# LayerNorm 1 to the first gather in token halves, with the routing ranked by comparison

## The reference

```python
mod = cond @ w_ada[l] + b_ada[l]              # sh1, sc1, gt1, sh2, sc2, gt2
...                                           # mixer: mLSTM heads and a short convolution
x = layer_norm(ALPHA * x + (1 + gt1) * mix, ln1_g[l], ln1_b[l])
u = x * (1 + sc2) + sh2
grp_logits = u @ w_grp + b_grp                # 4 groups
grp_idx = argmax(grp_logits)
exp_logits = u @ w_router + b_router          # 4 experts in each group
top_vals, top_idx = top_k(exp_logits[grp_idx], 2)
top_w = softmax(top_vals) * softmax(grp_logits)[grp_idx]
y = sum over the 2 experts of top_w * (silu(u @ w_gate) * (u @ w_up)) @ w_down
x = layer_norm(ALPHA * x + (1 + gt2) * y, ln2_g[l], ln2_b[l])
```

## Time and profile before

| | us |
|---|---|
| three runs | 889.2, 884.86, 888.09; median 888.09 |
| profiled execution | 891.73 |
| its span | 889.9 |
| PE busy | 825.8 (93%) |
| DVE busy | 338.7 (38%) |
| ACT busy | 100.2 (11%) |
| DMA moved | 299.29 MB, 336 GB/s over the span |
| mean granted TensorE clock | 0.958 |

### The profile page before, as it was taken

How to read it: one execution, slowest core, us unless ns; L and a number is a source line. 1 busy time by engine, 2 the same in 40 slices (tenths; PEclk the granted TensorE clock), 3 DMA queues, 4 the chain that set the end, 5 groups by cost and what they waited for, 6 DMA issues and landing times.

```text
span 889.9 us, 9042 instructions
## 1 busy us (share of the span) xinstructions
PE 825.8 (93%) x3753; PEld 439.6 (49%) x3753; DVE 338.7 (38%) x807; ACT 100.2 (11%) x222; POOL 28.4 (3%) x69
## 2 busy tenths in 40 slices
PE   5899999969999999999979999998799999999991
PEld 2585686445344443443347658745444443444330
DVE  0169848653121012110253985676521112101106
ACT  2111000012011110110111100001111101111010
POOL 2060000000000000000000000000000000000000
PEclk9999999969999999999969999997899999999996
DMA  8999994284999999999999699336399999999961
GB/s 301 390 343 387 387 332 178 94 355 158 389 411 414 414 414 410 415 414 412 394 387 395 244 385 376 115 148 244 149 387 413 414 414 409 415 414 414 410 259 49
DMA packets 90653, 299.29 MB, mean 336 GB/s; under 512 B 4152, under 2 KB 4440, under 8 KB 82416
## 3 DMA queue, kind: packets, MB, share of 16 engines
q1 hardware_dynamic: 86960, 291.60, 84.2%
q0 software_dynamic: 2592, 7.04, 2.1%
q10 hardware_dynamic: 1056, 0.03, 0.1%
HBM read 297.60 MB, written 1.05 MB: 336 GB/s over the span
## 4 chain that ended last, share of the span: by engine, by line
PE 84%; DVE 4%; DMA 4%; SPq 4%; issue 2%; ACT 1%; ACTq 0%; DVEq 0%
PE bank L548 23%; PE bank L506 16%; PE bank L572 12%; PE bank L535 7%; PE bank L713 6%; PE bank L523 6%; PE bank L592 6%; SPq L335 3%; DMA ring<-in_w_ada_dram 2%; DMA ring<-in_w_in_dram 2%; PE bank L455 1%; PE bank L479 1%; PE bank L556 1%; SPq L331 1%; ACT uT L795 1%
## 5 line engine op out<-in xcount | busy, mean ns | idle before, releaser
L506 PE MATMUL bank<-uT,ring 128*128 128x256 f32 x640 | 142.6, 384 | 0.5 <-DMA ring<-in_w_in_dram 0.5
L506 PEld LDWEIGHTS bank<-uT,ring 128*128 128x128 f32 x640 | 122.6, 193 | 21.2 <-issue 3.5
L548 PE MATMUL bank<-ring,qT 128*64 128x512 f32 x512 | 113.1, 594 | 2.8 <-issue 2.8
L572 PE MATMUL bank<-ring,hb 128*64 128x512 f32 x512 | 113.4, 595 | 1.4 <-ACT hb L821 1.4
L548 PE MATMUL bank<-ring,uT 128*64 128x512 f32 x512 | 112.7, 594 | 0.0
L572 PEld LDWEIGHTS bank<-ring,hb 128*64 128x64 f32 x512 | 35.3, 137 | 76.4 <-issue 74.6
L548 PEld LDWEIGHTS bank<-ring,qT 128*64 128x64 f32 x512 | 36.8, 137 | 70.9 <-issue 69.9
L548 PEld LDWEIGHTS bank<-ring,uT 128*64 128x64 f32 x512 | 36.0, 137 | 70.8 <-issue 68.5
L535 PEld LDWEIGHTS bank<-ccT,X 128*128 128x128 f32 x512 | 62.5, 198 | 13.4 <-issue 13.4
L535 PE MATMUL bank<-ccT,X 128*128 128x128 f32 x512 | 64.9, 286 | 0.0
L935 DVE SCALAR_TENSOR_TENSOR acc<-ring,cond,acc 128x512 f32<-128x512 f32 x84 | 63.1, 752 | 3.0
(11 more groups left out here) (227 smaller groups left out, 564.3 us busy)
## 6 DMA issues: line engine op xcount, KB each, us to landing
ring<-in_w_gate_dram SPq DMA_DIRECT2D x32, 2048.0 KB, 17.0
ring<-in_w_up_dram SPq DMA_DIRECT2D x32, 2048.0 KB, 16.3
ring<-in_w_down_dram SPq DMA_DIRECT2D x32, 2048.0 KB, 15.6
ring<-in_w_ada_dram SPq DMA_DIRECT2D x24, 2048.0 KB, 19.8
ring<-in_w_in_dram SPq DMA_DIRECT2D x14, 2048.0 KB, 18.9
ring<-in_w_out_dram SPq DMA_DIRECT2D x4, 2048.0 KB, 14.2
gate_row<-in_b_ada_dram POOLq DMA_DIRECT2D x4, 512.0 KB, 7.7
ln_g<-in_ln_g_dram POOLq DMA_DIRECT2D x4, 512.0 KB, 10.5
```

What stands on the lines that cost most here:

```text
L506: last = pe.matmul(bank[4 + (b0 + q) % 4][:, 0:SEQ], w[:, kc, q * P:(q + 1) * P], uT[:, kc, :], start=(kc == 0), stop=(kc == KC - 1))
L548: last = pe.matmul(bank[bk][CAP * j:CAP * (j + 1), :], xg[b][:, 4 * h + k, CAP * j:CAP * (j + 1)], ring[s[h]][:, 4 * j + k, :], start=(h = ...
L572: last = pe.matmul(bank[6 + half][CAP * j:CAP * (j + 1), :], hhT[:, f, CAP * j:CAP * (j + 1)], ring[s[h]][:, 4 * j + 2 * i + half, :], sta ...
```

## The change

- Extractions 4 and 5 go ahead of the head transposes, 8 and 9 between these and the output projection; `shift_scale` goes ahead of `residual_norm`.
- The last block of the output projection (tile 1, half 1) is made in two blocks of 256 columns, in banks 3 and 7; LayerNorm's `add` follows it in two rounds.
- Transposes, modulation, route matmuls and fold are done for tokens 0 to 127 and then for 128 to 255, the first half's in parts on ScalarE alone.
- The routing compares every logit with each of its row of four, ranks them by the counts, and makes the mask (bf16) from the ranks. What only the weights need (`dif`, scores, `best`) comes behind the dispatch matrix.
- Clearing of banks 0 to 3 and the extractions of gate 2 stand ahead of the wait for the mask; two position matmuls in bf16 replace three in float32.
- `disp` and `dispw` are one instruction each of 256 columns; `dispw` is `disp` times the weight. Positions count from 1, so one subtraction is gone.

```diff
@@ -694,6 +713,8 @@
                 pe.wait_ge(proj_dve, 8 * l + 8)
                 ada_extract(l, GATE1)
                 ada_extract(l, GATE1 + 1)
+                ada_extract(l, 4)
+                ada_extract(l, 5)
 
                 pe.wait_ge(h_ready, l + 1)
                 pe.wait_ge(gate_row_ready, 4 * l + 2)
...
@@ -704,41 +725,46 @@
                     if h % 2:
                         last.then_inc(hT_done, 1)
+                ada_extract(l, 8)
+                ada_extract(l, 9)
                 pe.wait_ge(hT_copied, 2 * (l + 1))
                 for half in range(2):
                     arrived(pe, l, WOUT_UNIT[half])
                     w = ring[slot(l, WOUT_UNIT[half])]
                     for t in range(T):
-                        for kc in range(KC):
-                            last = pe.matmul(bank[2 * t + half][:, :], mixT[:, kc, t * P:(t + 1) * P], w[:, kc, :],
-                                             start=(kc == 0), stop=(kc == KC - 1))
-                        last.then_inc(mix_done, 1)
-                for i in (4, 5, 8, 9):
-                    ada_extract(l, i)
-                pe.wait_ge(x_ready, 2 * T * l + T)
-                transpose_x(x_ready, 2 * T * l + 1, 1, rows_of)
-                pe.wait_ge(uT_act, 8 * l + 8)
+                        for to, cols in blocks_of(t, half):
+                            for kc in range(KC):
+                                last = pe.matmul(to, mixT[:, kc, t * P:(t + 1) * P], w[:, kc, cols],
+                                                 start=(kc == 0), stop=(kc == KC - 1))
+                            last.then_inc(mix_done, 1)
+                transpose_half(l, 0)
+                pe.wait_ge(mod_ready, 2 * l + 2)
+                clear_quarters(6)
+                pe.wait_ge(uT_act, 16 * l + 12)
+                pe.wait_ge(route_landed, 16 * 10 * DEPTH)
+                in_quarters(6, w_route_sb[:, l, :, :], logT_done, slice(0, P))
+                transpose_half(l, 1)
+                pe.wait_ge(logT_act, l + 1)
+                pe.matmul(bank[6][:, SEQ:SEQ + G + EXPERTS], quarters[:, 0:P], fold[:, :], start=True, stop=True)
+                pe.wait_ge(uT_act, 16 * l + 16)
                 pe.wait_ge(uT_dve, 8 * l + 8)
-                pe.wait_ge(route_landed, 16 * 10 * DEPTH)
-                in_quarters(6, w_route_sb[:, l, :, :], logT_done)
+                in_quarters(6, w_route_sb[:, l, :, :], logT_done, slice(P, SEQ))
+                pe.wait_ge(logT_dve, l + 1)
+                pe.matmul(bank[6][:, SEQ + 32:SEQ + 32 + G + EXPERTS], quarters[:, P:SEQ],
+                          fold[:, :], start=True, stop=True).then_inc(logit_done, 1)
                 for b in range(4):
                     pe.matmul(bank[b][:, :], zeros[:, 0:P], zeros[:, :], start=True, stop=False, skip_group_check=True)
-                pe.wait_ge(logT_copied, l + 1)
-                for t in range(T):
-                    last = pe.matmul(bank[6][:, SEQ + 32 * t:SEQ + 32 * t + G + EXPERTS], quarters[:, t * P:(t + 1) * P],
-                                     fold[:, :], start=True, stop=True)
-                last.then_inc(logit_done, 1)
-                pe.wait_ge(mask_ready, l + 1)
-                pe.matmul(bank[6][:, 0:EXPERTS], before[:, :], mask[:, 0, :], start=True, stop=True)
-                pe.matmul(bank[6][:, EXPERTS:2 * EXPERTS], ones[:, :], mask[:, 0, :], start=True, stop=False)
-                pe.matmul(bank[6][:, EXPERTS:2 * EXPERTS], before[:, :], mask[:, 1, :],
-                          start=False, stop=True).then_inc(pos_done, 1)
                 ada_extract(l, GATE2)
                 ada_extract(l, GATE2 + 1)
+                pe.wait_ge(mask_ready, l + 1)
+                pe.matmul(bank[6][:, 0:2 * EXPERTS], before[:, :], mask[:, :, :].rearrange("p t e -> p (t e)"),
+                          start=True, stop=False, skip_group_check=True)
+                pe.matmul(bank[6][:, EXPERTS:2 * EXPERTS], all_ones[:, :], mask[:, 0, :],
+                          start=False, stop=True, skip_group_check=True).then_inc(pos_done, 1)
                 gather(main, PAIRS * l, 0)
...
@@ -962,22 +1005,33 @@
+            def residual_norm(l, which):
+                    blocks = [(bank[2 * t + half][:, :], slice(0, COLS))]
+                        blocks = blocks_of(t, half)
+                    for i, (src, cols) in enumerate(blocks):
+                        if which == 0:
+                            dve.wait_ge(mix_done, 5 * l + 2 * half + t + i + 1)
+                        to = slice(half * COLS + cols.start, half * COLS + cols.stop)
+                        n = cols.stop - cols.start
+                        link(dve.tensor_tensor(tmp[:, 0:n], src, gate_row[:, to], ALU.mult))
+                        link(dve.scalar_tensor_tensor(out=X[:, t, to], in0=X[:, t, to], scalar=ALPHA,
+                                                      in1=tmp[:, 0:n], op0=ALU.mult, op1=ALU.add))
+                        if which == 0 and t == T - 1:
+                            for q in range(to.start // SEQ, to.stop // SEQ):
+                                last = dve.bn_stats(stats[:, t, q, :], X[:, t, q * SEQ:(q + 1) * SEQ])
+                        else:
+                            last = dve.bn_stats(stats[:, t, half, :], X[:, t, to])
+                        link(last)
+                    n = 4 if which == 0 and t == T - 1 else 2
+                    link(dve.bn_aggr(mv[:, t, :], stats[:, t, 0:n, :].rearrange("p a b -> p (a b)")))
...
@@ -1006,41 +1060,25 @@
+                two_of = slice(e0, e0 + 2) if isinstance(e0, int) else bass.ds(e0, 2)
+                dve.tensor_tensor(disp[b][:, :, :].rearrange("p t (e s) -> p t e s", e=2),
+                                  slots[:, :].unsqueeze(1).unsqueeze(1).to_broadcast([P, T, 2, CAP]),
+                                  pos[:, :, two_of].unsqueeze(3).to_broadcast([P, T, 2, CAP]), ALU.is_equal).then_inc(S.disp, 1)
+            def build_dispw(S, n, e0, b):
+                two_of = slice(e0, e0 + 2) if isinstance(e0, int) else bass.ds(e0, 2)
+                dve.wait_ge(S.disp, n + 1)
+                dve.tensor_tensor(dispw[b][:, :, :].rearrange("p t (e s) -> p t e s", e=2),
+                                  disp[b][:, :, :].rearrange("p t (e s) -> p t e s", e=2),
+                                  comb[:, :, two_of].unsqueeze(3).to_broadcast([P, T, 2, CAP]), ALU.mult).then_inc(S.dispw, 1)
+            def build(S, n, e0, b):
+                build_dispw(S, n, e0, b)
...
@@ -1201,63 +1239,73 @@
+                shift_scale(l)
+                residual_norm(l, 0)
+                modulate_half(l, 1, range(4, KC))
+                dve.wait_ge(logT_done, 2 * l + 2)
+                dve.tensor_copy(quarters[:, P:SEQ], bank[6][:, P:SEQ]).then_inc(logT_dve, 1)
+                el = logit[:, :, G:G + EXPERTS]
+                rows = logit[:, :, :].rearrange("p t (n e) -> p (t n) e", e=E)
+                N = T * (1 + G)
+                link(dve.tensor_tensor(ahead[:, :, :, :], rows.unsqueeze(2).to_broadcast([P, N, E, E]),
+                                       rows.unsqueeze(3).to_broadcast([P, N, E, E]), ALU.is_ge))
+                link(dve.tensor_tensor(ahead[:, :, :, :], ahead[:, :, :, :],
+                                       lower[:, :, :].unsqueeze(1).to_broadcast([P, N, E, E]), ALU.mult))
+                dve.tensor_reduce(rank[:, :, :], ahead[:, :, :, :], AX.X, ALU.add)
+                link(dve.tensor_reduce(behind[:, :, :], ahead[:, :, :, :].rearrange("p n i j -> p n j i"), AX.X, ALU.add))
+                link(dve.tensor_tensor(rank[:, :, :], rank[:, :, :], behind[:, :, :], ALU.subtract))
+                want = last_rank[:, :].unsqueeze(1).to_broadcast([P, N, E])
+                dve.scalar_tensor_tensor(out=two[:, :, :, :].rearrange("p t n e -> p (t n) e"), in0=rank[:, :, :], scalar=-1.0,
+                                         in1=want, op0=ALU.add, op1=ALU.is_le)
+                link(dve.tensor_tensor(first[:, :, :, :].rearrange("p t n e -> p (t n) e"), rank[:, :, :], want, ALU.is_equal))
+                group = first[:, :, 0, :].unsqueeze(3).to_broadcast([P, T, G, E])
+                dve.tensor_tensor(mask[:, :, :].rearrange("p t (g e) -> p t g e", g=G), two[:, :, 1:1 + G, :], group,
+                                  ALU.mult).then_inc(mask_ready, 1)
+                dve.wait_ge(mask_ready, l + 1)
+                dve.tensor_tensor(chosen1[:, :, :, :], first[:, :, 1:1 + G, :], group, ALU.mult)
+                link(dve.tensor_reduce(best[:, :, 0:1], gl, AX.X, ALU.max))
+                dve.tensor_tensor(dif[:, :, 0:G], gl, best[:, :, 0:1].to_broadcast([P, T, G]), ALU.subtract)
+                link(dve.tensor_tensor(chosen2[:, :, :, :], mask[:, :, :].rearrange("p t (g e) -> p t g e", g=G),
+                                       chosen1[:, :, :, :], ALU.subtract))
+                build_disp(main, 0, 0)
```

(61 more changed lines are left out.)

123 lines of the change are left out of this document (36 added, 87 removed).

## The result

The changed kernel takes 879.78 us (median of 20 runs, 875.79 to 889.67) against 883.62 us for the kernel before (20 runs). The ratio is 0.994, interval 0.9918 to 0.9962: 5.3 us faster (3.4 to 7.2). It leaves out two slow runs of the changed kernel and so is further from 1 than the ratio of the medians as they stand, which differ by 3.8 us. A second set gives 0.9935 (0.9906 to 0.9963), 5.8 us. The forecast was 10.5 us. The direction was right, but the gain is half of the forecast. That the time of 879.78 us lies even in the likeliest case's 874 to 880 is luck: the forecast started from the median of three runs, 888.09, and over 20 runs the kernel before has 883.62.

What follows compares the result with a forecast made beforehand. TensorE (busy 93%) was taken as the bound, except some 25 us per layer between output projection and gather. Gains of 7.75 and 7.4, less 2 x 2.25 and 0.1, gave 10.5 us: 877.6 from 888.09, range 873 to 884.

Steps and rivals of the forecast that it cites:

- the likeliest case: The whole kernel, no rival coming true: 877.6 us, own range 874 to 880, chance 0.64.
- Time saved here reaches the end: Between output projection and gather: a microsecond saved in either layer counts as one of the span.
- The extractions, +2.25 per layer: Extractions 4, 5, 8 and 9, moved ahead of the output projection, lengthen the path by 2.25 us per layer.
- The split: Last output projection block as 16 matmuls of 256 columns for 8 of 512: costs nothing, at most 0.1 us.
- the low clock at the projection: Rival: the clock falls near 150 and the projection's start runs at half; 3.4 us lost per layer, 884.4 us; chance 0.08.
- LayerNorm, logits, routing: M + 5.25, 10.9, 13.3: After the output projection's end (M): LayerNorm's X ready at 5.25 us, logits at 10.9, mask at 13.3.
- The 160-column steps: VectorE's routing ahead of the mask: two operations at 0.32 us, reductions 0.25 and 0.36, interpolated between measured rows; whole 2.4 us.
- The wait for the mask, gather at M + 17.3: TensorE's clearing and gate 2 extractions outlast the mask by 2.9 us; gather begins 17.3 us after the output projection's end.
- The sum: Both layers: 7.75 and 7.4 us gained, less 2 x 2.25 for extractions and 0.1 for the split: 10.5 us.
- Slower than before: Rival: longer low clock at the projection, and gather low too; 2.75 us slower per layer, 893.6 us; chance 0.04.
- the stream that doesn't move: Rival: transfers fixed elsewhere hold the passage between the layers, so layer 0 brings nothing; 882.8 us; chance 0.05.
- the low clock at the gather: Rival: the pause for positions and dispatch keeps the gather at low clock; 3.4 us per layer, middle 882.7 us; chance 0.14.

Runs made afterwards that it cites:

- 64 columns: The changed kernel with the 16 matmuls of extractions 4, 5, 8 and 9 of 64 columns in place of one; ratio to before 0.9869, second set 0.9863.

## Why the prediction was right, and where it missed

**Time saved here reaches the end.** Held as far as the traces show: behind the first gate matmul of layer 1 every trace takes 250.7 to 251.3 us more (one 252.1), and where layer 0's gate matmuls start at 207.86 in place of 208.74, layer 1's fourth ada unit starts at 453.37 in place of 454.35. The passage varies by up to 7.7 us with its clock, which the prediction did not reckon with.

**The extractions, +2.25 per layer.** Measured +1.86 at full clock (6.52 with 64 columns for 4.66), and +1.96 to +2.76 with one column in the changed kernel. The working was right to 0.4 us; the rest is the clock. That the first pair's two layers add up to the forecast 4.5 is chance: 3.7 of it is the work and 0.8 the low clock.

**The split, "nothing, at most 0.1".** The split itself costs nothing: 27.56 us with 64 columns. But the step took the projection's length as unchanged, and it grew by 1.4 to 2.5 us per layer, 3.8 and 4.7 over both in the changed kernel's two traces. This is the term that was mis-sized. The prediction had the mechanism as a rival of its own, the low clock at the projection, at a chance of 0.08 and 3.4 us per layer. Its argument against it, that the extractions stand between full matmuls and leave no pause, is refuted: no pause is needed. It had also named a clock of 0.50 in the projection as a sign of being wrong, and the sign came. The price was nearly right. Against 64 columns, extractions and projection together are 1.7 us longer in layer 0 of the first trace, where the clock is low for 3.4 us, and 3.3 in the other three, where it is low for 6.8. Only the chance was far too low: the clock fell in all twelve projections of the six traces that have one-column matmuls ahead (29.1 to 30.4 us). So the case that came is this rival's, and the forecast's range was met by the luck of the baseline named above and by stages that went better than forecast.

The Trainium skill ("TensorE: Matmul & The Clock Gate", section "Part 4: PE-mode transpose") says that the full clock doesn't engage for transposes, which don't count as busy in the same way. No run here tests that by itself. With 64 columns the clock stayed at 1.00 across the same eight transposes, 0.88 us of them, so that they alone did not decide here.

**LayerNorm, logits, routing: M + 5.25, 10.9, 13.3.** In layer 0 M is 186.0 and X is there at 191.27, M + 5.3; the logits at 196.93, M + 10.9; the mask at 199.34, M + 13.3. Layer 1 has M + 5.2, 10.8 and 13.2. All held. The 160-column steps took 0.32 us, as on the line through the rows; the reduction read crosswise took 0.42 for the 0.36 allowed.

**The wait for the mask, gather at M + 17.3.** Measured 16.3 to 16.7, since the last extraction already gained from the returning clock (2.86 for 3.60): 0.6 to 1.0 better than forecast. The reading that TensorE and not the mask ends the stage held: making the mask 2.1 us later cost 0.2 us over both layers.

**The sum.** Forecast 10.5; by the first traces 8.2, by the second 5.2. In the first pair the way to the projection grew by 4.5 over both layers, as forecast; the projection by 3.8 for 0.1; and its end to the gather fell by 16.7 for 15.1. In the terms of the prediction: 10.5, less 5.0 and 6.6 us for the low clock at the projection in the two changed traces, plus 1.2 for extractions at full clock that cost less, plus 1.6 and 0.4 for the stage behind the projection, gives 8.3 and 5.5. The 2.9 us between the first pair's stretches and the 5.3 measured over 20 runs are within what the stretches themselves vary (124.4 to 125.5 and 117.3 to 119.2). Slower than before, the stream that doesn't move, and the low clock at the gather didn't happen; the last one did as soon as gate 2 was taken from in front of it.

## What to carry to other kernels

Before moving small matmuls ahead of a long dense stretch, ask what they do to the granted clock and not only how long they are. Where the weight load sets the pace of a matmul, as here, try to make it wider: 64 columns in place of one cost nothing and kept the clock. When work is moved out of the place just ahead of a stretch, look whether it was what brought the clock back; and where the granted clock is low in many short waits, harmless matmuls in them may be worth more than a shorter chain on another engine; here they shortened the stretch by 5 to 7 us, and the total by nothing that is clear of its noise. Last, compare two traces part by part, with the granted clock of each part: parts that nobody edited differed by 5 to 8 us here.

## What was not expected of the hardware

A TensorE that is busy 100% of the time can be set back to 1.2 GHz. In the changed kernel, first trace, two groups of 16 records of one-column matmuls with 8 records of transposes between them were issued in some 5 us, and in the second group the clock fell to half: from 156.4 to 159.8 in layer 0 and from 576.2 to 583.1 in layer 1, 3.4 and 6.8 us. With 64 columns in place of one, 16 records take 1.83 us (1.77 to 1.94 with one in layer 0) and the clock stays at 2.4 GHz. Clearing matmuls on operands that are all zero hold it there as well: with them in TensorE's waits it is at 1.00 from 150 to 192 us and from 570 to 610 in all three traces.
